# A hybrid DeltaNet and sliding-window block on one core: low parts of 48 weight tiles and the masked decays made by VectorE instead of GpSimd

## The chip, the core and the metric

One core of a Trainium2 chip. The metric is the device time of one launch in microseconds (us), the median of the runs. The engines are named as the profile names them: PE (TensorE, matrix products), PEld (its weight loads), DVE (VectorE), ACT (ScalarE), POOL (GpSimd), SP (SyncE, which issues the large transfers).

## What is computed

One layer over 2048 positions of 1024 channels: an RMS norm, one projection of all branches, a gated delta rule with 8 heads in chunks of 64 positions, a sliding-window attention with 16 query heads, two output projections merged by gates, an output product, a residual and a last norm.

```
h = rms_norm(x, norm_w);  z = h @ w_in
qkv = silu(causal_depthwise_conv(cat[qa, ka, va], conv_w))
oa = gated_delta_rule(qa, ka, va, g, beta)      # per head: T = (I - N)^-1 by squarings, then a scan over chunks
oa = rms_norm(oa, gdn_norm_w) * silu(za);  ya = oa @ w_o_a
ob = swa_sink_attention(qb, kb, vb, sinks, bias) * silu(zb);  yb = ob @ w_o_b
x = x + (sigmoid(gate_a) * ya + sigmoid(gate_b) * yb) @ w_out
return rms_norm(x, final_norm_w)
```

Inside the delta rule, `decay` is exp of differences of summed decays; it is used once masked to the lower triangle (for q k) and once masked strictly and negated (for the matrix N).

## The kernel before, in words

**Blocks and heads.** The 2048 positions go in 4 blocks of 512 (`NB`, `TB`). A block has a short prologue, 8 heads (`head`), 16 gate tiles, 8 + 8 tiles of the output projections and 8 of the last product. While head h runs its scan, TensorE puts the projection of head h + 1 between the small products of head h, one contraction step of three products at a time (`fill(n)`; lines 1211 to 1213 are the three products of a step). In the last head of a block the first six gate tiles are the filling.

**Weight tiles.** The weights are 91 tiles of 128 x 1024 numbers. A product with a tile is made exact by splitting weight and activation in a high part (rounded to the fp32r format) and a low part (what is left), and adding three products: high by high, low weight by high, high weight by low. In the first block each tile is split on the chip, once: the raw tile is loaded into one of two slots of `w_raw` (SP, line 365), ScalarE copies it rounded into `w_sl` (line 480, the high part, semaphore `hi_ready`), GpSimd subtracts (line 401, the low part, `lo_ready`), and SP saves the pair to memory (line 375) and then loads the raw tile that is two further. The later blocks load the saved pairs (line 384), and split nothing. `w_sl` has three slots, so the high part of tile f is made when TensorE has finished tile f - 3 (`tile_done`) and that one's save has landed.

**Order.** Each engine runs a program written out by hand, in its own order; a wait in it holds everything behind it. Tiles are used in the order of their numbers f: 0 to 2 in the prologue, 3 to 50 for the eight heads (six each, the projections of q, k, v, the attention's q, and the two gates `za` and `zb`), 51 to 66 for the gate tiles, and so on. During head h of the first block TensorE works on tiles 9 + 6h to 14 + 6h. ScalarE makes high parts at fixed places in its own program (`refill`), right after it has read out the product that freed the slot.

**GpSimd in a head** (before): `rk` (a power of four numbers, line 414), the strictly masked decays `dec_n` (line 428), two low parts, the products `gu` for the next head's decays (line 420), two low parts, `rqo` (line 414), two low parts. Tiles 12 to 59 are split there, in the eight heads of the first block. In all 32 heads `dec_n` is made there.

**VectorE in a head:** it ends the head before with the gated norm (`za` scaled in line 1092, its high part 1095, its low part 1096), then the gates' SiLU of the head to come (`za`, `zb`, line 908), which frees the two banks that TensorE's next projection writes to. Then come `ssk`, the masked decays `dec_u` (line 957), the factor `kn` (line 960, needs `rk` of GpSimd), the matrix N (line 968, needs `dec_n`; it releases TensorE's transposes in line 1386), and the levels of the inversion. Then there are four scan steps t = 0 to 3:

```
dve: wait ks_done;  r_sb = bank5 * negc + vr        # L1054, releases L1427 of TensorE
     fill(1)  (not at t = 2)                        # convolution or SiLU of the next head
     wait ds_done;  s_cur = s_cur * e + bank6       # L1060, releases L1417 of TensorE's next step
     o_sb = bank7 + o1;  t = 0: fill(2);  t = 1: quotient(1), fill(1);  t = 2: fill(2)
```

TensorE's step is: L1417 and L1422 (products with the state), two steps of filling (three at t = 0), L1427 (needs `r_sb`), one step of filling, L1432 and L1435 (need ScalarE's copy `y_sb`, line 705), one step of filling. At t = 2 it transposes the attention's probabilities (line 1371) behind L1427; ScalarE copies them (line 689), copies the attention's q projection into `qbd` (lines 601 and 602), and then makes the next high part (line 480).

## Time and profile before

| what | value |
|---|---|
| median of the 3 runs shown | 2831.02 us (2830.4 to 2836.27) |
| the profiled execution's own time | 2835.45 us |
| its span, first to last instruction | 2833.6 us |
| PE busy in the span | 2783.0 us (98%) |
| DVE, ACT, POOL busy | 1406.3, 958.6, 450.7 us |
| chain that ended last | PE 92%, DVE 4%, ACT 1% |

The profile gives, for one execution, each engine's busy time, groups of instructions by source line, and what ended each idle stretch. A product is recorded as longer than the distance to the next one (they overlap), and ends are modelled, so a short wait of TensorE shows only in part as idle time. The sure measure of one is how long a stretch of identical work lasts. Such stretches are there: all four blocks do the same products, and only the first also splits weights.

### The profile page before, as it was taken

The numbers are of one execution on the slowest core, as the hardware profiler recorded it, in microseconds if no ns is written. First come the engines' busy times: TensorE is split into PE (matmuls) and PEld (weight loads), VectorE is DVE, ScalarE is ACT, GpSimd is POOL, SyncE is SP. The second block draws the span as 40 slices with busy tenths as digits, with TensorE's granted clock in tenths as the row PEclk, the third lists the DMA queues.
The fourth block names the chain that finished last, engine by engine and source line by source line (L and its number), as shares of the span: only waits on it lengthen the run. The fifth ranks groups of instructions, "written<-read, shape, count | busy, mean of one in ns | idle before, by whom it ended". The sixth has DMA issues, their size and how long they took to land.

```text
span 2833.6 us, 48983 instructions
## 1 busy us (share of the span) xinstructions
PE 2783.0 (98%) x19632; PEld 2288.2 (81%) x19632; DVE 1406.3 (50%) x3177; ACT 958.6 (34%) x2973; POOL 450.7 (16%) x272
## 2 busy tenths in 40 slices
PE   7999999999999999999999999999999999999998
PEld 6777777788888888888888888888888888888887
DVE  5676766513256666632326666652223666665112
ACT  4444444432234334331013434342111434343101
POOL 4333333343211100100001100100000100110000
PEclk9999999999999999999999999999999999999999
DMA  7444444488643333345554333335555333333454
GB/s 257 171 175 156 150 151 167 161 302 320 229 180 122 109 107 122 122 158 212 195 203 146 107 113 116 124 107 188 211 188 217 109 120 114 117 121 106 176 221 166
DMA packets 79568, 462.99 MB, mean 163 GB/s; under 512 B 13296, under 2 KB 17392, under 8 KB 31856
## 3 DMA queue, kind: packets, MB, share of 16 engines
q1 hardware_dynamic: 65808, 430.47, 42.4%
q10 hardware_dynamic: 13536, 29.40, 2.9%
q8 instruction: 157, 2.57, 0.4%
q14 instruction: 67, 0.55, 0.1%
HBM read 356.02 MB, written 103.81 MB: 162 GB/s over the span
## 4 chain that ended last, share of the span: by engine, by line
PE 92%; DVE 4%; ACT 1%; issue 1%; DMA 1%; POOL 1%; ACTq 0%; DVEq 0%; SPq 0%
PE bank L1211 24%; PE bank L1213 22%; PE bank L1212 22%; PE bank L1337 5%; PE bank L1326 3%; PE bank L1364 2%; PE bank L1311 2%; PE bank L1379 1%; PE bank L1371 1%; PE bank L1299 1%; PE bank L1427 1%; PE bank L1432 1%; PE bank L1417 1%; PE bank L1422 1%; PE bank L1435 1%
## 5 line engine op out<-in xcount | busy, mean ns | idle before, releaser
L1211 PE MATMUL bank<-hT_hi,w_sl 128*128 128x512 f32 x2144 | 909.2, 424 | 14.7 <-DVE za L908 13.8
L1213 PE MATMUL bank<-hT_hi,w_sl 128*128 128x512 f32 x2144 | 844.0, 394 | 0.0
L1212 PE MATMUL bank<-hT_lo,w_sl 128*128 128x512 f32 x2144 | 841.9, 393 | 0.0
L1211 PEld LDWEIGHTS bank<-hT_hi,w_sl 128*128 128x128 f32 x2144 | 406.2, 189 | 95.9 <-issue 27.5
L1213 PEld LDWEIGHTS bank<-hT_hi,w_sl 128*128 128x128 f32 x2144 | 404.7, 189 | 90.5
L1212 PEld LDWEIGHTS bank<-hT_lo,w_sl 128*128 128x128 f32 x2144 | 407.1, 190 | 59.9 <-issue 0.7
L401 POOL TENSOR_TENSOR w_sl<-w_raw,w_sl 128x1024 fp32r<-128x1024 f32 x91 | 229.5, 2525 | 436.0 <-ACT w_sl L480 435.9
L926 DVE SCALAR_TENSOR_TENSOR area<-zraw,stc,area 128x512 f32<-128x512 f32 x288 | 237.2, 823 | 3.3
L414 POOL TENSOR_TENSOR rqo<-qo,half 128x8 f32<-128x8 f32 x32 | 52.4, 1636 | 986.6 <-DVE qo L1077 986.6
L821 DVE TENSOR_SCALAR area<-bank 128x256 f32<-128x256 f32 (+1 forms) x192 | 81.0, 422 | 239.7 <-PE bank L1337 200.7
L1337 PE MATMUL bank<-area 64*64 64x128 f32 (+1 forms) x3072 | 162.4, 245 | 0.0
L1060 DVE SCALAR_TENSOR_TENSOR s_cur<-s_cur,scs,bank 128x128 f32<-128x128 f32 x128 | 44.3, 346 | 232.1 <-PE bank L1432 232.1
L652 ACT ACTIVATE area<-bank 128x256 f32<-128x256 f32 x160 | 61.4, 384 | 252.9 <-PE bank L1326 252.9
L1337 PEld LDWEIGHTS bank<-area 64*64 64x64 f32 x3072 | 134.7, 134 | 11.8 <-issue 11.8
L1326 PEld LDWEIGHTS bank<-area 64*64 64x64 f32 x2560 | 87.1, 134 | 59.8 <-issue 54.5
L480 ACT ACTIVATE w_sl<-w_raw 128x1024 fp32r<-128x1024 f32 x91 | 96.0, 1056 | 78.2 <-PE bank L1213 39.4
L575 ACT ACTIVATE zraw<-bank 128x512 f32<-128x512 f32 x96 | 56.5, 589 | 173.2 <-PE bank L1213 170.4
L570 ACT ACTIVATE area<-area 128x512 f32<-128x512 f32 x96 | 60.0, 625 | 153.0 <-DVE area L926 153.0
L1326 PE MATMUL bank<-area 64*64 64x64 f32 x2560 | 109.0, 224 | 1.7 <-ACT area L656 1.7
L414 POOL TENSOR_TENSOR sty<-sty,half 128x1 f32<-128x1 f32 (+1 forms) x7 | 7.1, 1020 | 612.9 <-DVE sty L1198 424.8
L702 ACT ACTIVATE o_sb<-bank,scs 128x128 f32<-128x128 f32 x128 | 46.5, 363 | 171.0 <-PE bank L1422 170.9
L1211 PE MATMUL bank<-oa_hi,w_sl 128*128 128x512 f32 x256 | 100.6, 393 | 0.0
(209 smaller groups left out, 4623.0 us busy)
## 6 DMA issues: line engine op xcount, KB each, us to landing
w_sl<-saved_w SPq DMA_DIRECT2D x273, 1024.0 KB, 4.8
saved_w<-w_sl SPq DMA_DIRECT2D x91, 1024.0 KB, 4.9
w_raw<-in_w_tiles SPq DMA_DIRECT2D x91, 512.0 KB, 6.0
area<-in_x ACTq DMA_DIRECT2D x4, 2048.0 KB, 10.5
area<-in_x ACTq DMA_DIRECT2D x14, 512.0 KB, 7.6
out_y<-area ACTq DMA_DIRECT2D x3, 2048.0 KB, 7.2
bias_sb<-in_bias ACTq DMA_DIRECT2D x32, 128.0 KB, 2.8
out_y<-area ACTq DMA_DIRECT2D x4, 512.0 KB, 2.9
```

Of the source, the lines that this page charges most:

```text
L401: pool.tensor_tensor(w_sl[:, s, 1, :], w_raw[:, f % 2, :], w_sl[:, s, 0, :].bitcast(F32), ALU.subtract).then_inc(lo_ready, 1)
L414: pool.tensor_tensor(dst, src, half[:, 0:n], ALU.pow).then_inc(ready, 1)
L480: act.activation(w_sl[:, s, 0, :], w_raw[:, f % 2, :], ACT.Copy).then_inc(hi_ready, 1)
L570: act.activation(ez[i % 2], qkv[:, par, i, :], ACT.Tanh, scale=0.5).then_inc(tanh_z[i], 1)
L652: act.activation(p_sb[l % 2], pv(bank[5]), ACT.Copy).then_inc(p_ready, 1)
L821: return dve.tensor_scalar(dst, src, 1.0, None, ALU.mult)
L926: ins = dve.scalar_tensor_tensor(acc, zraw[:, i, k:k + TB], stc[:, par, CONV * i + k:CONV * i + k + 1], acc, ALU.mult, ALU.add)
L1211: pe.matmul(dst, a_hi, b_hi, start=first, stop=False)
L1212: pe.matmul(dst, a_hi, b_lo, start=False, stop=False)
L1213: return pe.matmul(dst, a_lo, b_hi, start=False, stop=last)
L1326: ins = pe.matmul(pv(bank[5])[lo:hi, t, :], ptt[lo:hi, t, 0:CH], p_sb[(l - 1) % 2][lo:hi, t, :], start=True, stop=True)
L1337: ins = pe.matmul(bch(6)[lo:hi, t, c0:c1], p_sb[(l - 1) % 2][lo:hi, t, :], ptt[lo:hi, t, c0:c1], start=True, stop=True)
```

## The change

VectorE makes the low parts of tiles 12 to 59: six in each of the first block's eight heads, called `low(0)` to `low(5)`, of tiles 12 + 6h + j. They stand behind the third level of the inversion (0), behind the output of scan step 0 (1), behind `quotient(1)` in scan step 1 (2), behind `r_sb` in scan step 2, where `fill(1)` is left out (3), before the wait for the transposed output at the head's end (4), and at the very end (5). Each waits for the tile's high part (`hi_ready`) and for the low part before it (`lo_ready`). GpSimd keeps the tiles 0 to 11 and 60 to 90, with a wait for the low part before. The strictly masked decays `dec_n` are made by VectorE too, ahead of `dec_u`, in all 32 heads.

```
--- before.py
+++ after.py
@@ -27,6 +27,7 @@
 GATE_TILES = 2 * KT
 OUT_TILES = 8
 FILL_GATES = 6
+SCAN_LOWS = 12
 SLOTS = 3
 
 F32 = mybir.dt.float32
@@ -398,10 +399,12 @@
 
                 f, s = WEIGHT[n], n % SLOTS
                 pool.wait_ge(hi_ready, f + 1)
+                after(pool, lo_ready, f)
                 pool.tensor_tensor(w_sl[:, s, 1, :], w_raw[:, f % 2, :], w_sl[:, s, 0, :].bitcast(F32),
                                    ALU.subtract).then_inc(lo_ready, 1)
 
-            fresh = iter([n for n in range(len(USES)) if FRESH[n]])
+            fresh = iter([n for n in range(len(USES)) if FRESH[n]
+                          and not SCAN_LOWS <= WEIGHT[n] < SCAN_LOWS + H * HEAD_TILES])
 
             def low(count):
                 for _ in range(count):
@@ -424,17 +427,11 @@
             def head(h, n1, last):
 
                 power(rk[:, :], ssk[:, :], NT, ssk_ready, n1, rk_ready)
-                pool.wait_ge(dec_ready, n1)
-                pool.tensor_tensor(dec_n, dec, mk[:, NEGSTRICT:NEGSTRICT + 1, :].to_broadcast([P, NT, P]),
-                                   ALU.mult).then_inc(decn_ready, 1)
-                low(2)
                 if not last:
                     pool.wait_ge(dec_done, n1)
                     decays(h + 1, n1 + 1)
-                low(2)
                 power(rqo[:, :, :].rearrange("p a t -> p (a t)"), qo[:, :, :].rearrange("p a t -> p (a t)"), 2 * NT,
                       qo_ready, n1, rqo_ready)
-                low(2)
 
             power(st4[:, 4:8], st4[:, 8:12], NT, x_mean, 1, x_rstd)
             low(SLOTS)
@@ -941,8 +938,21 @@
                     yield from silu(i, bank[slot][:, :], dst[:, par, :], z_read[slot])
                 assert ch.k == DVE_PROJ, ch.k
 
+            def low_part(f):
+
+                n = WEIGHT.index(f)
+                dve.wait_ge(hi_ready, f + 1)
+                dve.wait_ge(lo_ready, f)
+                dve.tensor_tensor(w_sl[:, n % SLOTS, 1, :], w_raw[:, f % 2, :], w_sl[:, n % SLOTS, 0, :].bitcast(F32),
+                                  ALU.subtract).then_inc(lo_ready, 1)
+
             def head(b, hh, fill):
                 par, n1 = hh % 2, b * H + hh + 1
+
+                def low(j):
+                    if b == 0:
+                        low_part(SCAN_LOWS + hh * HEAD_TILES + j)
+
                 n4, n5, n6 = ((n1 - 1) * i for i in (NT, LEVELS, LEVELS + 1))
                 ch = Chain(dve, dve_head, (n1 - 1) * DVE_HEAD)
 
@@ -954,6 +964,7 @@
                 dve.wait_ge(ssq_ready[1], n1)
                 dve.tensor_scalar(ssk[:, :], ssq[:, 1, :], 4 * EPS, None, ALU.add).then_inc(ssk_ready, 1)
                 dve.wait_ge(dec_ready, n1)
+                dve.tensor_tensor(dec_n, dec, mk[:, NEGSTRICT:NEGSTRICT + 1, :].to_broadcast([P, NT, P]), ALU.mult).then_inc(decn_ready, 1)
                 ch.inc(dve.tensor_tensor(dec_u, dec, mk[:, UPTO:UPTO + 1, :].to_broadcast([P, NT, P]), ALU.mult))
                 dve.wait_ge(rk_ready, n1)
                 dve.wait_ge(ssk_ready, n1)
@@ -1036,6 +1047,7 @@
                 level(2)
                 logits(0)
                 level(3)
+                low(0)
                 fill(1)
                 level(4)
                 quotient(0)
@@ -1055,6 +1067,8 @@
                                              ).then_inc(r_ready, 1)
                     if t != 2:
                         fill(1)
+                    else:
+                        low(3)
                     dve.wait_ge(s_ready if t else s0_ready, n4 + t if t else n1)
                     dve.wait_ge(ds_done, n4 + (t + 1))
                     dve.scalar_tensor_tensor(s_cur[:, (t + 1) % 2, :], s_cur[:, t % 2, :], sc[:, EGL, t:t + 1], bank[6][:, 0:P],
@@ -1063,9 +1077,11 @@
                     dve.wait_ge(o1_ready, n4 + (t + 1))
                     dve.tensor_tensor(o_sb[:, t, :], bank[7][:, 0:P], o1_sb[:, t % 2, :], ALU.add).then_inc(o_ready, 1)
                     if t == 0:
+                        low(1)
                         fill(2)
                     elif t == 1:
                         quotient(1)
+                        low(2)
                         fill(1)
                     elif t == 2:
                         fill(2)
@@ -1086,6 +1102,7 @@
 
                 dve.tensor_tensor(o_sb, o_sb, fo[:, :, None].to_broadcast([P, NT, P]), ALU.mult).then_inc(on_ready, 1)
                 fill(2)
+                low(4)
                 dve.wait_ge(ot_done, n1)
                 dve.wait_ge(z_read[bank_of(za_n)], reads_before(za_n) + 1)
                 zat = za[:, par, :]
@@ -1096,6 +1113,7 @@
                 dve.tensor_tensor(oa_lo[:, hh, :], zat, oah.bitcast(F32), ALU.subtract
                                   ).then_inc(head_dve_done, 1)
                 fill(99)
+                low(5)
                 assert ch.k == DVE_HEAD, ch.k
 
             prologue(0)
```

GpSimd, from the low parts ahead of the first head to the second head, first before the change and then with it (in all order rows: `gu` the products for the decays, `area` or `area2` the scratch memory, `mk` the masks).

```order
L401 TENSOR_TENSOR w_sl<-w_raw,w_sl 128x1024 [waits hi_ready] x3
L414 TENSOR_TENSOR rk<-ssk,half 128x4 [waits ssk_ready]
L428 TENSOR_TENSOR area<-area,mk 128x512 [waits dec_ready]
L401 TENSOR_TENSOR w_sl<-w_raw,w_sl 128x1024 [waits hi_ready] x2
L420 TENSOR_TENSOR gu<-mk,g_hi 128x512 [waits g_split,sc_ready,dec_done]
L420 TENSOR_TENSOR gu<-mk,g_lo 128x512
L401 TENSOR_TENSOR w_sl<-w_raw,w_sl 128x1024 [waits hi_ready] x2
L414 TENSOR_TENSOR rqo<-qo,half 128x8 [waits qo_ready]
L401 TENSOR_TENSOR w_sl<-w_raw,w_sl 128x1024 [waits hi_ready] x2
```

```order
L403 TENSOR_TENSOR w_sl<-w_raw,w_sl 128x1024 [waits lo_ready,hi_ready] x3
L417 TENSOR_TENSOR rk<-ssk,half 128x4 [waits ssk_ready]
L423 TENSOR_TENSOR gu<-mk,g_hi 128x512 [waits g_split,sc_ready,dec_done]
L423 TENSOR_TENSOR gu<-mk,g_lo 128x512
L417 TENSOR_TENSOR rqo<-qo,half 128x8 [waits qo_ready]
```

The six low parts and the masked decays are gone from GpSimd's head, and what is left stands in the old order.

VectorE, scan steps 1 and 2 of a first-block head, before and with the change (`r_sb` and `s_cur` are the writes that release TensorE; `area1` holds the next head's convolutions; the row on `w_sl` is a low part).

```order
L1023 TENSOR_TENSOR den<-psum_row,esink 128x4 [waits exp_ready1]
L1024 RECIPROCAL rden<-den 128x4 [waits dve_head]
L1025 TENSOR_TENSOR area2<-area2,rden 128x512 [waits dve_head]
L908 SCALAR_TENSOR_TENSOR area1<-area2,area1 128x512 [waits tanh_z1]
L1054 SCALAR_TENSOR_TENSOR r_sb<-bank5,negc,area2 128x128 [waits ks_done]
L1060 SCALAR_TENSOR_TENSOR s_cur<-s_cur,scs,bank6 128x128 [waits ds_done,s_ready]
```

```order
L1034 TENSOR_TENSOR den<-psum_row,esink 128x4 [waits exp_ready1]
L1035 RECIPROCAL rden<-den 128x4 [waits dve_head]
L1036 TENSOR_TENSOR area2<-area2,rden 128x512 [waits dve_head]
L946 TENSOR_TENSOR w_sl<-w_raw,w_sl 128x1024 [waits lo_ready,hi_ready]
L905 SCALAR_TENSOR_TENSOR area1<-area2,area1 128x512 [waits tanh_z1]
L1066 SCALAR_TENSOR_TENSOR r_sb<-bank5,negc,area2 128x128 [waits ks_done]
L946 TENSOR_TENSOR w_sl<-w_raw,w_sl 128x1024 [waits lo_ready,hi_ready]
L1074 SCALAR_TENSOR_TENSOR s_cur<-s_cur,scs,bank6 128x128 [waits ds_done,s_ready]
```

One low part now stands ahead of step 2's `r_sb`, and one between it and the step's `s_cur`.

VectorE at the turn from one head to the next, before and with the change.

```order
L908 SCALAR_TENSOR_TENSOR area1<-area2,area1 128x512 [waits tanh_z2,zraw_free]
L1092 SCALAR_TENSOR_TENSOR za<-bank4,gnw,za 128x512 [waits z_read1,ot_done]
L1095 TENSOR_SCALAR oa_hi<-za 128x512 [waits ot_read]
L1096 TENSOR_TENSOR oa_lo<-za,oa_hi 128x512 [waits dve_head]
L908 SCALAR_TENSOR_TENSOR za<-area2,bank1 128x512 [waits tanh_z3]
L908 SCALAR_TENSOR_TENSOR zb<-area2,bank0 128x512 [waits tanh_z4]
L821 TENSOR_SCALAR s_cur<-s_all 128x128
```

```order
L905 SCALAR_TENSOR_TENSOR area1<-area2,area1 128x512 [waits tanh_z2,zraw_free]
L946 TENSOR_TENSOR w_sl<-w_raw,w_sl 128x1024 [waits lo_ready,hi_ready]
L1109 SCALAR_TENSOR_TENSOR za<-bank4,gnw,za 128x512 [waits z_read1,ot_done]
L1112 TENSOR_SCALAR oa_hi<-za 128x512 [waits ot_read]
L1113 TENSOR_TENSOR oa_lo<-za,oa_hi 128x512 [waits dve_head]
L905 SCALAR_TENSOR_TENSOR za<-area2,bank1 128x512 [waits tanh_z3]
L905 SCALAR_TENSOR_TENSOR zb<-area2,bank0 128x512 [waits tanh_z4]
L946 TENSOR_TENSOR w_sl<-w_raw,w_sl 128x1024 [waits lo_ready,hi_ready]
L818 TENSOR_SCALAR s_cur<-s_all 128x128
```

A low part stands ahead of the four instructions that end in the release of `za`'s bank, and one behind the two SiLUs.

## Rows read from the trace of the kernel before

**Rows 1.** Stretches: start:end, length, busy of PE, PEld, DVE, ACT, POOL, PEclk, DMA

```profile
77.20:498.30 421.10, 403.69 (x3348) 328.85 (x3346) 287.78 (x618) 194.99 (x614) 150.70 (x76) 0.98 0.46 160
804.40:1198.40 394.00, 394.00 (x3348) 324.25 (x3346) 246.27 (x619) 159.08 (x574) 45.02 (x35) 1.00 0.33 116
498.30:804.40 306.10, 299.94 (x1566) 246.57 (x1564) 103.42 (x174) 97.57 (x185) 104.10 (x46) 0.99 0.71 257
1198.40:1496.20 297.80, 297.32 (x1565) 245.66 (x1564) 85.18 (x174) 58.36 (x144) 8.95 (x7) 1.00 0.54 195
77.20:134.50 57.30, 56.52 (x480) 46.29 (x478) 38.39 (x84) 26.51 (x86) 18.90 (x10) 1.00 0.48 168
134.50:194.10 59.60, 56.75 (x480) 46.23 (x479) 42.73 (x89) 28.00 (x89) 21.96 (x11) 1.00 0.46 162
194.10:255.20 61.10, 58.38 (x482) 47.57 (x480) 41.08 (x89) 28.13 (x89) 21.93 (x11) 0.97 0.46 159
```

**Rows 2.** Groups of instructions by line (count, busy us, mean ns, idle before)

```profile
L401 POOL TENSOR_TENSOR w_sl<-w_raw,w_sl 128x1024 fp32r<-128x1024 f32 x91 | 229.5, 2525 | 436.0 <-ACT w_sl L480 435.9
...
L1427 PE MATMUL bank<-r_sb,area 128*128 128x128 f32 x256 | 51.9, 284 | 5.0 <-DVE r_sb L1054 5.0
```

**Rows 3.** Timeline, first block, turn to head 3 (start, length, instruction, idle before)

```profile
256.99 5.42 POOL L401 TENSOR_TENSOR w_sl<-w_raw,w_sl 128x1024 fp32r<-128x1024 f32 x2 [3.82 <-ACT w_sl L480]
...
257.44 2.73 DVE L1096 TENSOR_TENSOR oa_lo<-za,oa_hi 128x512 fp32r<-128x512 f32 x1
...
260.09 0.67 DVE L908 SCALAR_TENSOR_TENSOR za<-area,bank 128x512 f32<-128x512 f32 x1
...
260.91 0.47 PE L1211 MATMUL bank<-hT_hi,w_sl 128*128 128x512 f32 x1 [1.92 <-DVE za L908]
```

**Rows 4.** Timeline, second block, the same turn

```profile
860.00 0.58 ACT L611 ACTIVATE area<-bank 128x512 f32<-128x512 f32 x1
...
860.88 0.75 DVE L1092 SCALAR_TENSOR_TENSOR za<-bank,gnw,za 128x512 f32<-128x512 f32 x1
...
862.13 0.69 DVE L1096 TENSOR_TENSOR oa_lo<-za,oa_hi 128x512 fp32r<-128x512 f32 x1
862.73 0.68 DVE L908 SCALAR_TENSOR_TENSOR za<-area,bank 128x512 f32<-128x512 f32 x1
...
864.16 0.48 PE L1211 MATMUL bank<-hT_hi,w_sl 128*128 128x512 f32 x1
...
865.79 1.25 DVE L960 SCALAR_TENSOR_TENSOR kn<-rk,ssk 128x4 f32<-128x4 f32 x1 [0.90 <-POOL rk L414]
```

**Rows 5.** Timeline, first block, head 2, scan step 2 and into step 3

```profile
243.02 0.35 DVE L1054 SCALAR_TENSOR_TENSOR r_sb<-bank,negc,area 128x128 f32<-128x128 f32 x1
...
245.37 0.35 DVE L1060 SCALAR_TENSOR_TENSOR s_cur<-s_cur,scs,bank 128x128 f32<-128x128 f32 x1 [2.00 <-PE bank L1432]
...
246.02 0.38 PE L1417 MATMUL bank<-s_cur,area 128*128 128x128 f32 x2
246.09 1.06 ACT L480 ACTIVATE w_sl<-w_raw 128x1024 fp32r<-128x1024 f32 x1
```

**Rows 6.** Timeline, second block, `r_sb` and its reader in scan steps 1 and 2

```profile
900.64 0.35 DVE L1054 SCALAR_TENSOR_TENSOR r_sb<-bank,negc,area 128x128 f32<-128x128 f32 x1
...
901.21 0.38 PE L1427 MATMUL bank<-r_sb,area 128*128 128x128 f32 x2
...
904.70 0.35 DVE L1054 SCALAR_TENSOR_TENSOR r_sb<-bank,negc,area 128x128 f32<-128x128 f32 x1
...
905.10 0.49 PE L1427 MATMUL bank<-r_sb,area 128*128 128x128 f32 x2
```

**Rows 7.** Groups of VectorE in one head of the second block

```profile
L992 DVE TENSOR_TENSOR area<-bank,area 128x256 f32<-128x256 f32 x4 | 1.7, 417 | 0.2 <-PE bank L1337 0.2
...
L1095 DVE TENSOR_SCALAR oa_hi<-za 128x512 fp32r<-128x512 f32 x1 | 0.4, 426 | 0.0
```

**Rows 8.** DMA issues of the page (KB each, median us to landing)

```profile
w_raw<-in_w_tiles SPq DMA_DIRECT2D x91, 512.0 KB, 6.0
```

More of the change, by code:

```diff
@@ L29 @@
 FILL_GATES = 6
+SCAN_LOWS = 12
 SLOTS = 3
@@ L400, in low_part @@
                 pool.wait_ge(hi_ready, f + 1)
+                after(pool, lo_ready, f)
                 pool.tensor_tensor(w_sl[:, s, 1, :], w_raw[:, f % 2, :], w_sl[:, s, 0, :].bitcast(F32),
                                    ALU.subtract).then_inc(lo_ready, 1)
-            fresh = iter([n for n in range(len(USES)) if FRESH[n]])
+            fresh = iter([n for n in range(len(USES)) if FRESH[n]
+                          and not SCAN_LOWS <= WEIGHT[n] < SCAN_LOWS + H * HEAD_TILES])
             def low(count):
@@ L426, in head @@
                 power(rk[:, :], ssk[:, :], NT, ssk_ready, n1, rk_ready)
-                pool.wait_ge(dec_ready, n1)
-                pool.tensor_tensor(dec_n, dec, mk[:, NEGSTRICT:NEGSTRICT + 1, :].to_broadcast([P, NT, P]),
-                                   ALU.mult).then_inc(decn_ready, 1)
-                low(2)
                 if not last:
@@ L942, in project, with low_part, low @@
                 assert ch.k == DVE_PROJ, ch.k
+            def low_part(f):
+                n = WEIGHT.index(f)
+                dve.wait_ge(hi_ready, f + 1)
+                dve.wait_ge(lo_ready, f)
+                dve.tensor_tensor(w_sl[:, n % SLOTS, 1, :], w_raw[:, f % 2, :], w_sl[:, n % SLOTS, 0, :].bitcast(F32),
+                                  ALU.subtract).then_inc(lo_ready, 1)
             def head(b, hh, fill):
                 par, n1 = hh % 2, b * H + hh + 1
+                def low(j):
+                    if b == 0:
+                        low_part(SCAN_LOWS + hh * HEAD_TILES + j)
                 n4, n5, n6 = ((n1 - 1) * i for i in (NT, LEVELS, LEVELS + 1))
@@ L956, in head @@
                 dve.wait_ge(dec_ready, n1)
+                dve.tensor_tensor(dec_n, dec, mk[:, NEGSTRICT:NEGSTRICT + 1, :].to_broadcast([P, NT, P]), ALU.mult).then_inc(decn_ready, 1)
                 ch.inc(dve.tensor_tensor(dec_u, dec, mk[:, UPTO:UPTO + 1, :].to_broadcast([P, NT, P]), ALU.mult))
@@ L1038, in head @@
                 level(3)
+                low(0)
                 fill(1)
@@ L1057, in head @@
                         fill(1)
+                    else:
+                        low(3)
                     dve.wait_ge(s_ready if t else s0_ready, n4 + t if t else n1)
@@ L1065, in head @@
                     if t == 0:
+                        low(1)
                         fill(2)
@@ L1068, in head @@
                         quotient(1)
+                        low(2)
                         fill(1)
@@ L1088, in head @@
                 fill(2)
+                low(4)
                 dve.wait_ge(ot_done, n1)
@@ L1098, in head @@
                 fill(99)
+                low(5)
                 assert ch.k == DVE_HEAD, ch.k
```

2 lines of the change are left out of this document (removed).

## The prediction

> **What bounds the kernel now.** I read the stretches first, because all four blocks do the same products and only the first splits weights. From head 0 to head 7 the first block takes 421.10 us and the second 394.00, for the same 3348 products of TensorE. From head 7 to the next block's first head it is 306.10 against 297.80 [rows 1]. So the splitting costs the kernel 27.1 + 8.3 = 35.4 us, and that is all a change to it could give back. In the second block TensorE is busy for 394.00 of 394.00 us, so nothing that VectorE or GpSimd saves there can shorten it.
>
> Next, what the 35.4 us are. At the turn between heads TensorE sat idle until VectorE's SiLU of `za` [rows 3]. In the second block that SiLU comes 1.85 us after the scaling of `za` began, and TensorE starts its first projection unhindered [rows 4]. In the first block TensorE stands idle for 1.92 us, and what is late is `oa_lo`: 2.73 us [rows 3] where it takes 0.69 [rows 4]. It began while two low parts of GpSimd ran (256.99 to 262.41). The same two engines meet elsewhere in the scan, and `r_sb` comes late for L1427 once per head of the first block: 5.0 us in all over eight heads, some 0.6 each [rows 2]. In some heads TensorE's granted clock falls behind the turn: head 1 lasts 59.60 us at 1.00, head 2 lasts 61.10 at 0.97, a stay at 1.2 instead of 2.4 GHz that costs 1.5 us [rows 1]. Of the seven heads behind a turn five read 0.97 and two 1.00. Head 0, at whose start none of this happens, lasts 57.30 [rows 1]; less the 0.6 us of its late `r_sb`, that leaves 0.4 us over a second-block head (394.00 / 7 = 56.3) for ScalarE's high parts, which stay.
>
> **What is removed.** 48 of the 91 low parts, at 2.5 us each [rows 2], leave GpSimd, which waited for them anyway (436 us idle for high parts). What this gives is the end of the collisions: up to the whole 35.4 us, less 8 x 0.4 for the high parts, so 32 us.
>
> **What is added.** VectorE subtracts 128x512 numbers in 0.69 us, and the next instruction starts 0.60 behind it [rows 4]. A tensor_tensor of 256 numbers takes 0.42 [rows 7], so 256 more cost 0.27 and 512 more 0.54: a low part of 1024 delays what is behind it by 0.60 + 0.54 = 1.14 us. It is bounded below by the one-input copy (0.43 us for 512 [rows 7], so some 0.7) and above by twice the whole 0.69, 1.4. I take 1.14, from the row of the same operation. Six per head are 6.8 us, beside some 19 us in which VectorE is idle per head (421.10 - 287.78, over 7 [rows 1]). Room there is; what matters is the place of each.
>
> - `low(0)`: behind the third level, where VectorE waits for TensorE afterwards. Nothing.
> - `low(1)`: ahead of `r_sb` of step 1. That began at 900.64 and would begin at 901.78, ending 902.13, where TensorE's L1427 is ready at 901.21 [rows 6]. **0.95 us.**
> - `low(2)`: ahead of `r_sb` of step 2, whose end (905.05) L1427 already follows at 905.10 [rows 6]. No slack: **1.1 us.** The collision that made it 0.7 late is gone, and is counted in the 35.4.
> - `low(3)`: here the wait costs more than the work. It is tile 15 + 6h, in head 2 tile 27. Its high part was made from 246.09 to 247.15, at ScalarE's fixed place behind the `qbd` copies, and these wait for a transpose that itself comes after this step's L1427. VectorE reaches `low(3)` at 243.3, right behind `r_sb` (243.02), and would stand until 247.2. Then 1.14 us, so `s_cur` begins at 248.33 and not at 245.37 [rows 5]. Step 3's L1417, at 246.02 with 0.3 us of slack, waits **2.7 us.** Queued behind the wait are `s_cur`, `o_sb`, two convolution pieces and the `r_sb` of step 3. The distances from L1427 to the high part are all on TensorE and ScalarE, so the stall moves along with any delay before it.
> - `low(4)`: ahead of the scaling of `za`. Its high part comes behind ScalarE's tanh of `za` (860.00, 0.58 long, in the second block's frame), so from 860.5 to 861.55 with its 1.06 us [rows 5]. The low part starts at 861.6, the scaling at 862.71 instead of 860.88, the SiLU at 864.56, and TensorE's projection at 865.3 instead of 864.16 [rows 4]. **1.1 us**, in place of 1.92.
> - `low(5)`: behind both SiLUs; it delays `ssk` and with it `rk`. In exchange `kn`, 1.25 us long next to the `dec_n` of GpSimd [rows 4], falls to the 0.16 of its size. N then ends some 0.3 us before TensorE's L1386 wants it. Nothing, with little to spare.
> - `dec_n` on VectorE, 32 times 0.60 us, fits in the 0.90 us in which it waits for `rk` [rows 4]. Nothing, in any block.
> - SP: the raw tile f + 2 is loaded when low part f is there. Tile 27 is loaded behind `low(1)`, which ends before 901.8 in the second block's frame. Landed 6.0 us after [rows 8], at 907.8, it is there before its high part's place: 904.70 for step 2's `r_sb`, 0.95 + 1.14 later by the change, and 3.07 more from there (243.02 to 246.09), 909.9. If that cover went, each us of lateness would come on top of `low(3)`'s stall.
>
> Per head 1 to 6: 0.95 + 1.1 + 2.7 + 1.1 + 0.4 = 6.25 us. Head 0 has no such turn: 5.15. In head 7 VectorE has no convolutions and the high parts come sooner; I take 3. Sum 5.15 + 37.5 + 3 = 45.7 us against 35.4, so **+10 us**. To this come the falls of the clock, five of which are inside the old 35.4. They followed stalls of 1.9 us behind the turn's transposes; stalls of 1.1 there, and of 2.7 amid large products, I take to give two or three, +4 us. Together +14: 2849 for the profiled execution (2835.45), which lies 4.4 above the median; from the median, 2845 us.
>
> **Two rules of the skill.** VectorE's `oa_lo` grew by 2.04 us beside a GpSimd low part [rows 3, 4]. The Trainium skill ("SBUF — State Buffer", SBUF: two separate sides) says that VectorE operations with two SBUF inputs and GpSimd share one pair of ports, which the first comer holds for its whole instruction. By that rule `rk`, which GpSimd makes while VectorE is in `dec_u`, could also be held behind `dec_n` and `dec_u` back to back, 0.6 us longer; N would then come 0.3 us too late in each of seven heads, and the sum would be +16, not +14.
>
> The low part's price I took from `oa_lo` at 0.69 us for 512 [rows 4], not from the copy at 0.43 [rows 7]. The Trainium skill ("VectorE: DVE Perf Modes", The perf-mode tier table) holds that an fp32 tensor_tensor stays at one element per cycle; by that rule 1024 elements at its 0.96 GHz are an estimated 1.07 us of streaming. Its lower alternative is the second rival below.
>
> **The rivals.**
>
> 1. *Faster: the low parts fit in the idle time.* If tile 15 + 6h had its high part before VectorE gets there, `low(3)` would lie in the 2.00 us in which VectorE waits for L1432 [rows 5], and 7 x 2.7 = 19 us go: 2831 + 14 - 19 = 2826, or 2822 without the clock. If steps 1 and 2 take theirs as well, another 14 us: 2808; all of it would be 2799. It decides at a high part that ends before 244.2 in head 2. For it: 19 idle us per head against 6.8. Against: the high part ended at 247.15, behind work of step 2 itself. Chance 0.13.
> 2. *No change: a low part at the copy's pace.* 0.7 instead of 1.14 us saves 0.45 at each of four places, 7 x 1.8 = 13 us: 2832. Against: the row of the same form. Chance 0.09.
> 3. *Slower still.* If every 2.7 us stall is followed by a lower clock, seven times 1.5 us in place of the 4 taken is +6.5; with a low part at 1.4 us, 0.26 us more at four places of seven heads is +7: up to 2859. For it: five of seven turns fell before. Against: no fall followed the smaller waits inside the scan. Chance 0.17.
>
> **The numbers.** My forecast has 0.61, at 2845 (2837 to 2851). Runs of this kernel tell 0.2%, 5.7 us, from no change. Slower: 0.61 + 0.17 = 0.78. Same: the second rival, 0.09. Faster: 0.13, below the range. The range goes from 2832 to 2859. It takes in the second and third rivals and leaves out the first and the tails of the rest.
>
> **What would show it.** In the first block, the stretch from head 0 to head 7 near 440 us instead of 421 (394 + 5.15 + 37.5 + 4), and the one behind it near 301 instead of 306; the second block at 394 as before; GpSimd idle but for its powers and `gu`. VectorE's third scan low part should begin right behind a high part of ScalarE, with 3.9 us of idle time before it, and L1417 of step 3 should wait for `s_cur`. `oa_lo` back at 0.69 and `kn` at 0.16 would show the collisions gone. I am wrong if the wait before `low(3)` is short, or if the second block changes.

## The result, and the profile after

| | before | after |
|---|---|---|
| median | 2830.71 us (2830.31 to 2836.27) | 2854.55 us (2852.93 to 2858.09) |
| profiled execution: own time, span | 2835.45, 2833.6 us | 2855.0, 2853.2 us |
| after / before | | 1.0081 (95%: 1.0064 to 1.0099) |

The change makes the kernel 24 us slower. The forecast was 2845, so its sign and its whole range (2832 to 2859) hold, but it was 9.6 us too low. The time lies above the 2837 to 2851 that the forecast claimed for itself, in the part of the range that belonged to the third rival (more falls of the clock, chance 0.17).

The first view is the same four stretches as in [rows 1], now of the changed kernel: head 0 to head 7 of the first block, the same of the second, then head 7 to the next block's first head in both. Columns: window, length, busy us (with count) of PE, PEld, DVE, ACT and POOL, granted clock, DMA share, GB/s.

```profile
75.00:521.70 446.70, 408.70 (x3348) 329.69 (x3346) 290.55 (x666) 196.27 (x616) 40.92 (x30) 0.98 0.45 153
521.70:823.60 301.90, 298.14 (x1565) 245.46 (x1564) 101.47 (x183) 96.60 (x183) 83.21 (x37) 1.00 0.73 260
823.60:1217.50 393.90, 393.88 (x3346) 324.25 (x3345) 239.51 (x626) 159.31 (x574) 36.25 (x28) 1.00 0.32 116
1217.50:1515.40 297.90, 297.42 (x1566) 245.71 (x1565) 84.75 (x175) 58.44 (x145) 7.68 (x6) 1.00 0.54 195
```

The first stretch went from 421.10 to 446.70 (+25.6) and the one behind it from 306.10 to 301.90 (-4.2). The second block did not move. Head 0 starts at 75.0 instead of 77.2, in code that the change does not touch; this start varies between 74.8 and 77.4 in the runs below. These three, 25.6 - 4.2 - 2.2, make 19.2 of the 19.6 us between the two spans. GpSimd is busy for 40.92 us of the scan, VectorE for 290.55: the work went where it was meant to go, and TensorE stood idle for longer.

What TensorE waited for in the first block's heads (the view of waits; us in total, times, longest). The change shifts the line numbers: L1435, L1445, L1450, L1229, L1344 and L1404 are the L1417, L1427, L1432, L1211, L1326 and L1386 of the kernel before, and VectorE's L1066 and L1074 are its L1054 and L1060.

```profile
PE bank L1435 <- DVE s_cur L1074: 17.7, 7, 2.5
PE bank L1445 <- DVE r_sb L1066: 12.7, 15, 1.0
PE bank L1229 <- DVE za L905: 6.9, 7, 1.2
PE bank L1450 <- ACT y_sb L702: 2.2, 2, 1.4
PE bank L1344 <- ACT area L653: 2.0, 7, 0.3
PE bank L1404 <- DVE area L979: 0.2, 1, 0.2
```

The same view of the kernel before:

```profile
PE bank L1211 <- DVE za L908: 13.8, 7, 2.2
PE bank L1427 <- DVE r_sb L1054: 5.0, 8, 1.7
PE bank L1326 <- ACT area L656: 1.7, 6, 0.3
PE bank L1432 <- ACT y_sb L705: 1.4, 1, 1.4
PE bank L1386 <- DVE area L968: 0.9, 2, 0.4
```

The wait at the turn has halved, and that for `r_sb` now comes twice per head instead of once. The wait for `y_sb` belongs to head 7 in both kernels. A new one leads the list: in each of seven heads the product with the state waits for `s_cur`. Its cause shows in the timeline from step 2 to step 3 of head 2, the place of [rows 5]. Columns: start, duration, engine, line, operation; in brackets the idle time before it and its releaser.

```profile
248.81 0.34 DVE L1066 SCALAR_TENSOR_TENSOR r_sb<-bank,negc,area 128x128 f32<-128x128 f32 x1
...
249.20 0.49 PE L1445 MATMUL bank<-r_sb,area 128*128 128x128 f32 x2 [0.95 <-DVE r_sb L1066]
...
251.87 1.06 ACT L477 ACTIVATE w_sl<-w_raw 128x1024 fp32r<-128x1024 f32 x1
...
252.96 1.23 DVE L946 TENSOR_TENSOR w_sl<-w_raw,w_sl 128x1024 fp32r<-128x1024 f32 x1 [3.81 <-ACT w_sl L477]
...
254.10 0.34 DVE L1074 SCALAR_TENSOR_TENSOR s_cur<-s_cur,scs,bank 128x128 f32<-128x128 f32 x1
...
254.49 0.49 PE L1435 MATMUL bank<-s_cur,area 128*128 128x128 f32 x2 [2.53 <-DVE s_cur L1074]
```

VectorE has nothing left to do at 249.15, but its next instruction in order is `low(3)`, whose high part ScalarE finishes at 252.93. So VectorE stands for 3.81 us with `s_cur` queued behind, subtracts, and TensorE's L1435 waits for 2.53. Of the 15 waits for `r_sb` each of heads 0 to 6 has two, in steps 1 and 2; the one of step 2 is seen here, 0.95.

At the turn to head 3, the place of [rows 3]:

```profile
263.63 1.05 ACT L477 ACTIVATE w_sl<-w_raw 128x1024 fp32r<-128x1024 f32 x1
...
264.72 1.23 DVE L946 TENSOR_TENSOR w_sl<-w_raw,w_sl 128x1024 fp32r<-128x1024 f32 x1 [0.67 <-ACT w_sl L477]
...
265.86 0.74 DVE L1109 SCALAR_TENSOR_TENSOR za<-bank,gnw,za 128x512 f32<-128x512 f32 x1
...
267.10 0.69 DVE L1113 TENSOR_TENSOR oa_lo<-za,oa_hi 128x512 fp32r<-128x512 f32 x1
...
270.32 0.68 DVE L967 TENSOR_TENSOR area<-area,mk 128x512 f32<-128x512 f32 x1
...
270.49 1.38 POOL L417 TENSOR_TENSOR rk<-ssk,half 128x4 f32<-128x4 f32 x1 [9.54 <-DVE ssk L965]
270.92 0.68 DVE L968 TENSOR_TENSOR area<-area,mk 128x512 f32<-128x512 f32 x1
...
271.90 0.16 DVE L971 SCALAR_TENSOR_TENSOR kn<-rk,ssk 128x4 f32<-128x4 f32 x1 [0.30 <-POOL rk L417]
```

`oa_lo` is back at 0.69 us, `kn` at 0.16. `low(4)` takes 1.23 us and the scaling of `za` starts 1.14 behind it. The two groups of the page that stand for the work itself:

```profile
L946 DVE TENSOR_TENSOR w_sl<-w_raw,w_sl 128x1024 fp32r<-128x1024 f32 x48 | 58.5, 1219 | 33.4 <-ACT w_sl L477 33.4
L1113 DVE TENSOR_TENSOR oa_lo<-za,oa_hi 128x512 fp32r<-128x512 f32 x32 | 22.2, 693 | 1.1
```

Finally two neighbouring heads, 1 and 2:

```profile
136.50:200.90 64.40, 58.88 (x481) 47.51 (x479) 41.99 (x97) 28.13 (x90) 5.25 (x4) 0.97 0.44 150
200.90:263.80 62.90, 57.36 (x482) 46.30 (x480) 42.06 (x97) 28.20 (x90) 5.26 (x4) 1.00 0.45 154
```

They do the same work; one has the clock at 0.97 and is 1.5 us longer. The seven heads last 61.54, 64.38, 62.83, 64.39, 64.41, 64.39 and 64.76 us. Heads 1, 3, 4, 5 and 6 have the clock fall once, each time in step 3, behind the wait for `s_cur`. In head 1, for instance, L1435 starts at 190.09 after its wait, and the granted clock halves at about 191.3; in the other four it falls 0.3 to 1.4 us behind L1435's start. None has it at the turn.

Against the second block's head of 56.3 us, TensorE's products shift by these amounts in each head: 0.96 at step 1's `r_sb`, 1.12 at step 2's, 2.69 at step 3's L1435, 1.22 at the turn and 0.35 at L1344. (The idle times of the waits, 2.53 at L1435 for instance, are a little smaller than the shifts, since products are recorded as overlapping.) Head 0 has the first three (4.8), heads 1 to 6 all five (6.34 each, 38.0), the turn to head 7 the last two (1.5), and five falls cost some 1.6 each (8): 52.3, where the stretches differ by 446.70 - 393.90 = 52.8.

### The profile page after: what moved, and what is told of

Same layout as the page of the kernel before. It is cut to its first block, busy times and chain, and to the rows that moved or that the text cites. A ratio compares the mean times of both kernels' runs of the same rounds, so it can differ in the third digit from the quotient of the medians.

```text
span 2853.2 us, 49072 instructions
## 1 busy us (share of the span) xinstructions
PE 2783.4 (98%) x19632; PEld 2286.2 (80%) x19632; DVE 1386.9 (49%) x3257; ACT 959.5 (34%) x2973; POOL 288.1 (10%) x192
## 4 chain that ended last, share of the span: by engine, by line
PE 89%; DVE 3%; ACT 2%; issue 2%; DMA 1%; POOL 0%; DVEq 0%; ACTq 0%; SPq 0%
PE bank L1229 23%; PE bank L1231 22%; PE bank L1230 21%; PE bank L1355 5%; PE bank L1344 3%; PE bank L1382 2%; PE bank L1329 2%; PE bank L1397 1%; PE bank L1445 1%; PE bank L1389 1%; PE bank L1317 1%; PE bank L1450 1%; PE bank L1435 1%; PE bank L1440 1%; ACT w_sl L477 1%
## 5 line engine op out<-in xcount | busy, mean ns | idle before, releaser
L1229 PE MATMUL bank<-hT_hi,w_sl 128*128 128x512 f32 x2144 | 908.6, 424 | 7.7 <-DVE za L905 6.9
L1229 PEld LDWEIGHTS bank<-hT_hi,w_sl 128*128 128x128 f32 x2144 | 405.0, 189 | 87.7 <-issue 20.1
L923 DVE SCALAR_TENSOR_TENSOR area<-zraw,stc,area 128x512 f32<-128x512 f32 x288 | 224.1, 778 | 3.3
L1074 DVE SCALAR_TENSOR_TENSOR s_cur<-s_cur,scs,bank 128x128 f32<-128x128 f32 x128 | 44.4, 347 | 229.6 <-PE bank L1450 229.6
L1344 PEld LDWEIGHTS bank<-area 64*64 64x64 f32 x2560 | 87.1, 134 | 60.1 <-issue 54.5
L403 POOL TENSOR_TENSOR w_sl<-w_raw,w_sl 128x1024 fp32r<-128x1024 f32 x43 | 105.5, 2454 | 152.6 <-ACT w_sl L477 152.5
L1344 PE MATMUL bank<-area 64*64 64x64 f32 x2560 | 109.0, 224 | 2.0 <-ACT area L653 2.0
L1229 PE MATMUL bank<-oa_hi,w_sl 128*128 128x512 f32 x256 | 100.6, 393 | 0.3 <-DMA w_sl<-saved_w 0.3
L1229 PE MATMUL bank<-w_sl,oa_hi 128*128 128x512 f32 x256 | 100.5, 393 | 0.0
```

What stands on the lines that cost most here:

```text
L403: pool.tensor_tensor(w_sl[:, s, 1, :], w_raw[:, f % 2, :], w_sl[:, s, 0, :].bitcast(F32), ALU.subtract).then_inc(lo_ready, 1)
L923: ins = dve.scalar_tensor_tensor(acc, zraw[:, i, k:k + TB], stc[:, par, CONV * i + k:CONV * i + k + 1], acc, ALU.mult, ALU.add)
L1229: pe.matmul(dst, a_hi, b_hi, start=first, stop=False)
L1344: ins = pe.matmul(pv(bank[5])[lo:hi, t, :], ptt[lo:hi, t, 0:CH], p_sb[(l - 1) % 2][lo:hi, t, :], start=True, stop=True)
```

## Experiments

Eight kernels, in two sittings. The kernel before, run beside them, had a median of 2833.46 us in the first sitting (the first four below) and 2832.75 in the second; beside the changed kernel it had 2830.71. So a difference to the change's 2854.55 can be off by 2 to 3 us, while the ratios, and the stretches of the profiled executions, are free of this. Edits are against the changed kernel unless said otherwise.

### `low(3)` one step later

```
                                              ).then_inc(r_ready, 1)
+                    if t == 3:
+                        low(3)
                     if t != 2:
                         fill(1)
-                    else:
-                        low(3)
```

> The change with one low part moved: the fourth (tile 15 + 6h) goes from scan step 2, ahead of s_cur, to step 3, behind r_sb. Theory (the places of the low parts cost, above all the fourth, whose high part comes 3.7 us after VectorE is there): step 3's L1417 no longer waits 2.7 us in seven heads, -19 us, and the five falls of the clock that stood right behind these waits go too, -8 us: 2825 to 2831. A waiting time of the fourth low part of nearly 0, no new wait of TensorE in step 3. Rival (it is VectorE's total work that costs, 48 x 1.2 us, wherever it stands): 2850 to 2855. Second rival (the falls of the clock come from the heads' turns): 2834 to 2837, with the clock still at 0.996.

Measured: 2829.09 us (2827.95 to 2830.43), 0.9987 of the kernel before (0.9978 to 0.9995), so 25.5 us less than the change. Head 0 to head 7, in the view of stretches:

```profile
75.20:494.60 419.40, 399.34 (x3348) 323.71 (x3346) 290.81 (x666) 196.15 (x616) 42.99 (x30) 1.00 0.47 163
```

And step 3 of one head:

```profile
305.20 1.06 ACT L477 ACTIVATE w_sl<-w_raw 128x1024 fp32r<-128x1024 f32 x1
306.14 0.34 DVE L1066 SCALAR_TENSOR_TENSOR r_sb<-bank,negc,area 128x128 f32<-128x128 f32 x1
...
306.40 1.22 DVE L946 TENSOR_TENSOR w_sl<-w_raw,w_sl 128x1024 fp32r<-128x1024 f32 x1
...
308.38 0.35 DVE L1074 SCALAR_TENSOR_TENSOR s_cur<-s_cur,scs,bank 128x128 f32<-128x128 f32 x1
```

The high part ends at 306.26, the low part starts at 306.40 without a wait, and `s_cur` is still not late for TensorE. The subtraction is the same one; only its place in VectorE's order differs. The other waits are as large as before, the clock is 1.00, and no head shows a fall. The wait is 7 x 2.7 = 18.9 us and the five falls that followed it are about 8, together 26.9. The stretch is 446.70 - 419.40 = 27.3 shorter; the medians give 25.5, within what the sittings leave open. So the falls belong to the 2.7 us wait and not to those of 1.2 us at the turn. It also makes the change a gain of 0.13%, which the measurement does not tell from none by the 0.2% set ahead.

### `low(1)` into step 0's own gap

```
                     if t != 2:
                         fill(1)
                     else:
                         low(3)
+                    if t == 0:
+                        low(1)
...
                     if t == 0:
-                        low(1)
                         fill(2)
```

> The change with one low part moved: the second (tile 13 + 6h) goes from behind scan step 0's output, ahead of step 1's r_sb, to step 0, ahead of s_cur, where VectorE waits 2.7 us for TensorE. Theory: the 0.96 us that L1427 of step 1 waits in seven heads go, -6.7 us: 2846 to 2849. Rival (total work): 2854 as before.

Measured: 2846.49 us (2844.11 to 2848.17), ratio 1.0049 (1.0035 to 1.0063), 8.1 less than the change.

```profile
76.40:513.60 437.20, 405.14 (x3346) 328.75 (x3346) 290.38 (x666) 196.08 (x616) 40.10 (x30) 0.98 0.45 155
```

The waits for `r_sb` fall from 15 to 8, 7.1 us in all, and every other wait stays. That is 7 x 0.96 = 6.7 us. The stretch is 9.5 shorter; one fall fewer in it, four instead of five, makes 1.6 more, and 1.2 are not accounted for. A fifth fall comes in head 7 here. The term `low(1)` has the size forecast for it.

### All low parts at places with slack: `refit`

In addition to the last two edits `low(2)` moves from behind `quotient(1)` in step 1 to the place that `low(3)` left in step 2, and `low(4)` from before the wait for the transposed output to the end of the head.

```
+                    if t == 3:
+                        low(3)
                     if t != 2:
                         fill(1)
                     else:
-                        low(3)
+                        low(2)
+                    if t == 0:
+                        low(1)
...
                         quotient(1)
-                        low(2)
                         fill(1)
...
                 fill(2)
-                low(4)
                 dve.wait_ge(ot_done, n1)
...
                 fill(99)
+                low(4)
                 low(5)
```

> The change with five low parts moved to where VectorE waits for TensorE and the high part is there: the second to step 0 ahead of s_cur, the third to step 2 ahead of s_cur, the fourth to step 3 behind r_sb, the fifth behind both SiLUs at the turn, next to the sixth. Theory (place is all): the waits of 0.96, 1.12 and 2.7 us inside the scan and of 1.2 us at the turn go, 4.8 + 6 x 6.0 + 1.6 = 42 us, the falls of the clock too (8 us), and some 0.15 us per head comes back at L1386: 2802 to 2810, faster than both. Rival (total work of VectorE costs): 2845 to 2855. Rival (with the waits gone the loads of raw tiles become late): between 2815 and 2830, with ScalarE's high parts waiting for DMA.

Measured: 2817.56 us (2816.63 to 2820.58), ratio 0.9951 (0.9938 to 0.9963).

```profile
74.90:482.40 407.50, 397.00 (x3348) 324.93 (x3347) 291.31 (x666) 197.03 (x616) 41.25 (x30) 1.00 0.48 167
482.40:789.20 306.80, 301.15 (x1566) 247.62 (x1564) 103.85 (x183) 96.78 (x183) 83.30 (x37) 0.99 0.71 256
```

It is faster than both kernels, but 11 us short of what I expected: each head has a new wait of 0.9 to 2.0 us.

```profile
259.56 1.06 ACT L477 ACTIVATE w_sl<-w_raw 128x1024 fp32r<-128x1024 f32 x1 [1.65 <-DMA w_raw<-in_w_tiles]
...
262.47 0.68 PE L1346 MATMUL bank<-area 64*64 64x64 f32 x16 [1.66 <-ACT area L653]
```

SP loads the raw tile two further only when a low part is there. `low(4)` at the end of the head is late, so the raw tile lands 1.65 us after ScalarE wants it. ScalarE stands in its own order, and the copy that releases L1346 is behind. In head 7, where the steps are shorter, one of ScalarE's high parts comes late too, having waited 1.48 us for its load, and holds the `y_sb` copy, for which TensorE waits 3.02 us. So the late load, named in the expectation as the way it could fail, is what happened. The profiled execution also has the lower clock in two places, behind a 1.91 us wait of L1346 and in head 7.

### `dec_n` back to GpSimd, behind `rk`

```
                 power(rk[:, :], ssk[:, :], NT, ssk_ready, n1, rk_ready)
+                pool.wait_ge(dec_ready, n1)
+                pool.tensor_tensor(dec_n, dec, mk[...NEGSTRICT...], ALU.mult).then_inc(decn_ready, 1)
...
                 dve.wait_ge(dec_ready, n1)
-                dve.tensor_tensor(dec_n, dec, mk[...NEGSTRICT...], ALU.mult).then_inc(decn_ready, 1)
```

> The change without its second half: the strictly masked decays are made by GpSimd again, in all heads; the low parts stay where the change put them. Theory: kn is held up by the masked decays again (1.25 us instead of 0.16), N comes 1.1 us later, of which TensorE's L1386 had 0.3 us to spare in heads 1 to 7 and more than 1 us in blocks 2 to 4; the 0.35 us at L1326 is hidden by it. So +0.5 to +0.8 us in seven heads, 2858 to 2860. Rival (the masked decays are hidden everywhere, on either engine): 2854.5, no change.

Measured: 2860.88 us (2859.86 to 2862.03), ratio 1.0101 (1.0088 to 1.0115), 6.3 above the change.

```profile
76.50:528.20 451.70, 411.81 (x3348) 331.75 (x3346) 293.83 (x659) 196.75 (x616) 48.08 (x37) 0.97 0.44 150
830.60:1224.70 394.10, 394.10 (x3346) 324.16 (x3346) 246.95 (x619) 159.31 (x574) 45.07 (x35) 1.00 0.32 116
```

The products with N come 0.75 us later in heads 1 to 7 (this replaces the 0.35 at L1344), and seven heads instead of five have a fall, though the wait for `s_cur` is the same (17.7 us in seven times). The two together would be 7 x 0.4 + 2 x 1.6 = 6 us, where the stretch is 5.0 longer. The expectation, 2858 to 2860, had the 0.4 but not the two falls. So beside the low parts on VectorE, `dec_n` on VectorE is worth something in the first block; in the second block (394.10 against 393.90) next to nothing.

### `dec_n` alone on VectorE

All low parts go back to GpSimd; only the other part of the change stays. GpSimd's program in a head is then `rk`, two low parts, `gu`, two low parts, `rqo`, two low parts, and all calls of `low` in VectorE's program are gone.

```
-SCAN_LOWS = 12
...
-                after(pool, lo_ready, f)
...
                 power(rk[:, :], ssk[:, :], NT, ssk_ready, n1, rk_ready)
+                low(2)
...
-                low(0)
```

> The kernel before with the second half of the change alone: VectorE makes the strictly masked decays in all 32 heads, GpSimd keeps all low parts. Theory: VectorE makes them in the 0.9 us in which it waits for rk, kn is no longer held up, and N is 1.1 us earlier; TensorE gets from it only the 0.57 us that L1386 waited in heads 1 and 4 of the first block, and nothing in blocks 2 to 4: 2830 to 2834, no change that can be told. Rival (N is on the path in every head): 32 x 1.1 us less, 2800.

Measured: 2832.84 us (2827.77 to 2835.13) beside 2832.75 of the kernel before, ratio 0.9999 (0.999 to 1.0007).

```profile
77.20:499.40 422.20, 405.00 (x3346) 330.04 (x3345) 281.42 (x625) 195.20 (x614) 141.94 (x69) 0.98 0.47 160
```

Nothing, in the second block (393.80) or the first: the 1.1 us over the 421.10 before go with one more fall of the clock in this stretch, five instead of four. The forecast's "nothing" for `dec_n` holds.

### The kernel before, with GpSimd's low parts off the turn

Is it GpSimd's low parts that make VectorE late at the turn? Here, from head 1 on, GpSimd makes four low parts behind `dec_n`, and none behind `rqo` in heads 0 to 6, so none runs at the end of a head. The edit is against the kernel before.

```
-                low(2)
+                low(2 if h == 0 else 4)
                 if not last:
...
                       qo_ready, n1, rqo_ready)
-                low(2)
+                if last:
+                    low(2)
```

> The kernel before with GpSimd's order changed and nothing moved to VectorE: the last two low parts of heads 0 to 6 come behind rk and dec_n of the next head, off the turn where they held up oa_lo by 2 us. Theory of the collision alone: the 1.92 us at the turn go in seven heads with the clock falls behind them, -13 to -20 us: 2813 to 2820. My own expectation, from the late loads seen in the refit: these two low parts become some 8 us later, the raw tile for the high part at L1326 lands 3 to 5 us after ScalarE wants it, and what the turn gives is lost again: 2833 to 2848. In either case oa_lo takes 0.69 us instead of 2.73.

Measured: 2850.27 us (2848.95 to 2851.41), ratio 1.0062 (1.0048 to 1.0076), 2 us above my own expectation and far from what the collision alone would give. The timeline of a turn and of the start of the next head:

```profile
134.83 0.69 DVE L1097 TENSOR_TENSOR oa_lo<-za,oa_hi 128x512 fp32r<-128x512 f32 x1
...
137.08 1.01 POOL L414 TENSOR_TENSOR rk<-ssk,half 128x4 f32<-128x4 f32 x1 [6.51 <-DVE ssk L956]
...
139.31 4.69 POOL L401 TENSOR_TENSOR w_sl<-w_raw,w_sl 128x1024 fp32r<-128x1024 f32 x2
139.47 2.25 DVE L963 TENSOR_TENSOR bj<-rk,scs 128x4 f32<-128x4 f32 x1
...
141.75 2.27 DVE L965 TENSOR_TENSOR ksc<-bj,scs 128x4 f32<-128x4 f32 x1
...
147.99 1.06 ACT L481 ACTIVATE w_sl<-w_raw 128x1024 fp32r<-128x1024 f32 x1 [5.35 <-DMA w_raw<-in_w_tiles]
```

`oa_lo` takes 0.69 us and the wait of L1211 is gone: the collision was the cause of that wait. But it has moved on. `bj` and `ksc`, four numbers per partition, take 2.25 and 2.27 us, each as long as one of the two low parts that run beside them (4.69 together). In the kernel before they take 0.16 each. TensorE waits 23.4 us in eight heads for N, the longest 3.2. The Trainium skill ("SBUF — State Buffer", SBUF: two separate sides) has VectorE operations with two SBUF inputs and GpSimd share one pair of ports that is held for a whole instruction; by that rule the size of VectorE's operation does not matter, and these two rows agree. The loads come late as well, one 5.35 us behind ScalarE's want of it. So with GpSimd's low parts kept, this other place for them does not help: there they meet two small instructions of VectorE that TensorE's next products hang on.

### `refit` without its turn

`refit`, with `low(4)` left before the wait for the transposed output.

```
                 fill(2)
+                low(4)
                 dve.wait_ge(ot_done, n1)
...
                 fill(99)
-                low(4)
                 low(5)
```

(against `refit`)

> The first refit with the fifth low part left where the change has it, ahead of the scaling of za: it takes back one of the five moves. Theory: the 1.2 us at the turn are back in seven heads, but the raw tiles are loaded in time, and L1326 waits 0.35 us as with the change: heads 1 to 6 at 57.8 to 57.9 us, about what the refit has; 2814 to 2819, the same as the first refit within 3 us. Rival (the turn is the only thing that differs): 8 us slower than the refit, 2826.

Measured: 2815.12 us (2814.56 to 2815.53), ratio 0.9939 (0.9927 to 0.9952).

```profile
77.40:481.10 403.70, 396.02 (x3348) 324.36 (x3347) 290.24 (x666) 196.08 (x616) 40.38 (x29) 1.00 0.49 167
```

The late load of `refit` is gone from the heads (head 7 keeps its wait for `y_sb`, 3.0 us, and a fall), the turn's 1.20 us and L1346's 0.35 are back: 7 x 1.55 = 10.9 us, where the stretch is 403.70 - 393.90 = 9.8 above the second block's. `low(4)` at its old place costs about what it cost by the late load at the other.

### `refit2`: the SiLU first, then `low(4)`

Against `refit`: `low(4)` goes back before the wait for the transposed output, but the SiLU of the gate comes before it (`fill(3)` for `fill(2)`), since that is what TensorE waits for. In head 7, which has no convolutions, `low(2)` and `low(3)` stand where their high parts are there.

```
+                    end = hh == H - 1
-                    if t == 3:
+                    if t == 3 and not end:
                         low(3)
                     if t != 2:
                         fill(1)
                     else:
-                        low(2)
+                        low(3 if end else 2)
                     if t == 0:
                         low(1)
+                    elif t == 1 and end:
+                        low(2)
...
-                fill(2)
+                fill(3)
+                low(4)
                 dve.wait_ge(ot_done, n1)
...
                 fill(99)
-                low(4)
                 low(5)
```

> The refitted placement, mended at two places that its trace showed: at a head's turn the SiLU of za now comes first, then the fifth low part, then the scaling of za (it came behind both SiLUs, 2.4 us later, and the next raw tile was loaded that much later: ScalarE's high part for tile 12 + 6h began as the load landed, and TensorE's L1326 waited 0.9 to 2.0 us in heads 1 to 7); and in head 7 the third and fourth low parts stand one step earlier (TensorE's L1432 waited 2.5 us there). Theory (what is left of the first block's excess is the loads made late by late low parts): 7 x 1.1 us and one clock fall from the heads, some 5 us from head 7: 2802 to 2808. Rival (ScalarE's high parts themselves hold L1326 up): 2812 to 2818, no change against the first refit.

Measured: 2804.41 us (2801.76 to 2805.2), ratio 0.99 (0.9887 to 0.9914): 28 us less than the kernel before, 50 less than the change.

```profile
74.80:471.90 397.10, 395.40 (x3348) 323.82 (x3346) 290.51 (x666) 196.28 (x616) 41.66 (x30) 1.00 0.49 172
471.90:771.00 299.10, 297.57 (x1565) 245.56 (x1563) 101.86 (x183) 97.08 (x183) 83.32 (x37) 1.00 0.73 263
```

The turn to head 4:

```profile
301.17 1.05 ACT L477 ACTIVATE w_sl<-w_raw 128x1024 fp32r<-128x1024 f32 x1
...
301.50 0.68 DVE L905 SCALAR_TENSOR_TENSOR za<-area,bank 128x512 f32<-128x512 f32 x1
...
302.25 1.23 DVE L946 TENSOR_TENSOR w_sl<-w_raw,w_sl 128x1024 fp32r<-128x1024 f32 x1
...
303.40 0.75 DVE L1114 SCALAR_TENSOR_TENSOR za<-bank,gnw,za 128x512 f32<-128x512 f32 x1
```

The SiLU `za` is done at 302.18, while ScalarE makes the high part, and the low part starts right as that ends. The list of TensorE's waits in the first block's heads has two entries left, 1.4 and 1.3 us in all. Of the 35.4 us that splitting cost the kernel before, 3.2 + 1.2 = 4.4 are left (397.10 and 299.10 against 393.90 and 297.90). The 48 subtractions themselves, 58.5 us of VectorE, cost almost nothing when each stands where its input is ready and nothing waits behind it.

## Why the prediction was right, and where it was off

**What bounds it.** Right. The second block stayed at 393.90 us, and the 35.4 us were all that the change could give: `refit2` gets 31 of them.

**Removed: the collisions.** Right. `oa_lo` 2.73 to 0.69 us, `kn` 1.25 to 0.16; `pool_lows_off_turn` shows by itself that the low parts of GpSimd made the wait at the turn.

**`low(0)`, `low(5)`, `dec_n`: nothing.** Right: no wait there but one of 0.2 us at L1404, and `decn_alone` gives 0.9999.

**`low(1)`, 0.95 us.** The forecast's own rows give 902.13 - 901.21 = 0.92. Measured 0.96, and removed alone by `low1_in_step0`. **`low(2)`, 1.1 us:** 1.12. **The price of a low part, 1.14 us:** the next instruction starts 1.14 behind (264.72 to 265.86), so the second rival is out. The estimate from the Trainium skill ("VectorE: DVE Perf Modes", The perf-mode tier table), 1.07 us of streaming at one element per cycle, fits both: 0.07 below the delay of 1.14, and 0.15 below the recorded 1.22.

**`low(3)`, 2.7 us.** Measured 2.69, with 3.81 us of waiting for the high part where 3.9 were forecast. `low3_in_step3` removed it alone. Thus the first rival was wrong about this kernel and right about another: its 2826 with `low(3)` taken at 0 is 2829.09 in `low3_in_step3`, and its 2799 for "all of it" is 2804.41 in `refit2`.

**`low(4)`, 1.1 us.** Measured 1.22. **`rk` held longer.** Not by the change. By the rule of the Trainium skill ("SBUF — State Buffer", SBUF: two separate sides) `rk` could have been held behind `dec_n` and `dec_u` back to back, 0.6 more. It took 1.38 us (270.49), which is also its mean in the first block of the kernel before, where `dec_u` alone ran beside it. Held until the end of `dec_u`, 271.60, and then at the 1.01 us that it takes when it starts first, it would have ended at about 272.6 and not at 271.87. VectorE's wait for it fell from 0.90 to 0.30, and L1404 waited in one head for 0.2. The sum without the rule was the right one.

**Head 7, 3 us.** Too low by two and a half: 1.5 for its turn, and 4.0 for the rest (301.90 against 297.90). In the view of waits 0.4 of the rest is for `r_sb` and 2.2 for `y_sb`; one of the two waits for `y_sb` (0.82, before 570.60) stands behind a high part for which ScalarE waited 3.85 us, until its raw tile had landed. The kernel before waited 1.4 for `y_sb` there, and 1.7 of its 5.0 us for `r_sb` were in head 7 as well, so "some 0.6 each" was 0.5 in the other heads. I had not laid out that head's order; `refit2`, which does, gets 2.8 of it back.

**The clock: the term that was too small.** The forecast took "two or three" falls, +4, placed "there" and "amid large products". There were five, 8 us, all behind the 2.7 us waits. Beside a row in which five of seven turns had a fall behind 1.9 us, a wait of 2.7 should have been priced like them: the third rival had this, and its seven falls were nearer than my two or three. The forecast's 440 for the first stretch is 446.70: 4 by the falls, 1.5 by the turn to head 7, which I had booked to head 7.

**From the profiled execution to the median.** I took 4.4 us off, since that run of the kernel before was above its median. The change's profiled execution, 2855.0, is 0.5 above its own. That is 4 of the 9.6 us. The other 5.6 are the 14 us of the forecast against the 19.6 between the spans; the terms themselves were 7 too low (4 by the falls, 2.5 by head 7, the rest small), and head 0's earlier start, which nobody forecast, hid 2.2 of it. The difference between executions goes with the clock. The kernel before, run in the first sitting, has a mean granted clock of 0.998 in its fastest execution (2828.37) and of 0.994 in its slowest (2836.97), with some 2 us for each 0.001 in between. The profiled one had 0.996. So the number of falls most likely differs from one execution to the next, and a forecast that counts them in one execution cannot be surer than that.

## What to carry to other kernels

Price a moved instruction by the moment its inputs are there against the moment its engine's order reaches it, and by what stands behind it: the same 1.14 us of subtraction cost 2.7 us, 1.1 us or nothing, by place. When work on a second engine slows the first, taking it over can pay, but the places have to be chosen on the trace of the first: first serve the instruction that someone waits for, then fill, and see that the queue which loads the next input does not wait for the filling. And look whether a stall has a lower clock behind it: it added 8 us to 19.
